# Attention in a two-block fp32 model: transposed weight groups in pairs and in two banks, at four places of a round in place of eight

## The reference

```
for i in range(S // BLOCK_Q):                       # S = 512, BLOCK_Q = 128: four query blocks
    z = einsum('bhqd,bhkd->bhqk', qb, kb) * SB_SCALE  # keys 0 .. (i+1)*128
    log_1m_beta = where(mask, -softplus(z), 0.0)
    suffix = cumsum(log_1m_beta, reverse) - log_1m_beta
    w = where(mask, exp(log_sigmoid(z) + suffix), 0.0)
    outs.append(einsum('bhqk,bhkd->bhqd', w, vb))
p_a = (attn * silu(z_a)) @ w_branch_a
```

## Time and profile before

| what | value |
|---|---|
| median of 3 runs | 1523.73 us (1523.71 to 1523.83) |
| the profiled execution, its own time | 1523.92 us |
| its span, first to last instruction | 1522.2 us |
| TensorE matmul busy | 1507.5 us, 99% of the span |
| VectorE, ScalarE busy | 1014.8 us (67%), 713.3 us (47%) |
| attention rounds | from about 977.8 to 1215.3 us of the span |
| length of one looped round | 29.78 us (first score matmul of a round at 1036.51, of the next at 1066.29) |

### The profile page before, as it was taken

The page is one execution under the profiler, slowest core; times in us unless marked ns, Lnnn a source line. Parts: engine busy times, 40 slices in busy tenths (PEclk is TensorE's granted clock), DMA queues, the critical chain, the costliest instruction groups (busy, mean ns, idle before and its releaser), DMA issues.

```text
span 1522.2 us, 22929 instructions
## 1 busy us (share of the span) xinstructions
PE 1507.5 (99%) x8868; PEld 1334.1 (88%) x8868; DVE 1014.8 (67%) x1206; ACT 713.3 (47%) x1045; POOL 54.3 (4%) x101
## 2 busy tenths in 40 slices
PE   8999999999999999999999999999999999999998
PEld 7899998889888889899999888788888888888887
DVE  5888884327856848888886675688888775323243
ACT  6545443226566327544443324566766633312234
POOL 1000000002100002000000001000000000000001
PEclk9999999999999999999999999999999999999999
DMA  6233324322332231333325762232322222332321
GB/s 197 84 112 107 97 73 139 105 88 84 85 95 75 83 111 56 111 98 98 104 89 221 232 208 57 56 84 55 83 66 72 81 85 84 112 110 84 109 83 56
DMA packets 134909, 153.23 MB, mean 101 GB/s; under 512 B 3600, under 2 KB 123532, under 8 KB 134844
## 3 DMA queue, kind: packets, MB, share of 16 engines
q1 hardware_dynamic: 131584, 137.38, 28.8%
q0 software_dynamic: 3024, 14.88, 2.9%
q10 hardware_dynamic: 236, 0.06, 0.0%
HBM read 150.08 MB, written 2.23 MB: 100 GB/s over the span
## 4 chain that ended last, share of the span: by engine, by line
PE 96%; DVE 2%; ACT 1%; issue 0%; DMA 0%; DVEq 0%; ACTq 0%
PE ps L2305 21%; PE ps L2307 21%; PE ps L2306 21%; PE ps L2504 16%; PE ps L2509 8%; PE ps L2668 1%; PE ps L2769 1%; PE ps L2779 1%; PE ps L2753 1%; PE ps L2752 1%; PE ps L2778 1%; PE ps L2386 0%; PE ps L2735 0%; PE ps L2446 0%; DVE wl L1415 0%
## 5 line engine op out<-in xcount | busy, mean ns | idle before, releaser
L2305 PE MATMUL ps<-ah,wh 128*128 128x512 f32 (+1 forms) x1344 | 512.7, 381 | 3.1 <-DVE al L1469 1.2
L2307 PE MATMUL ps<-ah,wl 128*128 128x512 f32 (+1 forms) x1344 | 503.7, 375 | 0.0
L2306 PE MATMUL ps<-al,wh 128*128 128x512 f32 (+1 forms) x1344 | 503.1, 374 | 0.0
L2305 PEld LDWEIGHTS ps<-ah,wh 128*128 128x128 f32 x1344 | 253.4, 189 | 49.5 <-issue 2.3
L2307 PEld LDWEIGHTS ps<-ah,wl 128*128 128x128 f32 x1344 | 252.9, 188 | 46.0
L2306 PEld LDWEIGHTS ps<-al,wh 128*128 128x128 f32 x1344 | 253.4, 189 | 41.5
L1415 DVE TENSOR_TENSOR wl<-raw,wh 128x2048 fp32r<-128x2048 f32 x52 | 119.1, 2291 | 164.7 <-ACT wh L788 164.5
L788 ACT ACTIVATE wh<-raw 128x2048 fp32r<-128x2048 f32 x53 | 101.3, 1912 | 197.0 <-PE ps L2307 193.3
L2504 PE MATMUL ps<-ah,wh 128*128 128x256 f32 x576 | 141.3, 283 | 0.0
L2504 PE MATMUL ps<-al,wh 128*128 128x256 f32 x576 | 141.3, 283 | 0.0
L2504 PEld LDWEIGHTS ps<-al,wh 128*128 128x128 f32 x576 | 110.6, 192 | 0.1
(11 more groups left out here) (395 smaller groups left out, 2383.5 us busy)
## 6 DMA issues: line engine op xcount, KB each, us to landing
raw<-in_w_ffn_in SPq DMA_DIRECT2D x74, 512.0 KB, 3.5
raw<-in_w_ffn_out SPq DMA_DIRECT2D x22, 1024.0 KB, 5.0
raw<-in_w_in SPq DMA_DIRECT2D x36, 512.0 KB, 5.1
raw<-in_w_in SPq DMA_DIRECT2D x14, 1024.0 KB, 5.6
ada_raw<-in_w_ada POOLq DMA_DIRECT2D x8, 1536.0 KB, 7.1
raw<-in_w_mix_in SPq DMA_DIRECT2D x10, 1024.0 KB, 5.3
raw<-in_w_ffn_in SPq DMA_DIRECT2D x7, 1024.0 KB, 5.2
raw<-in_w_mix_out SPq DMA_DIRECT2D x4, 1024.0 KB, 4.9
```

The costliest lines, as they stand in the source:

```text
L2305: nc.tensor.matmul(bank, w[0], m[0], start=start, stop=False, skip_group_check=shared)
L2306: nc.tensor.matmul(bank, w[0], m[1], start=False, stop=False, skip_group_check=shared)
L2307: return nc.tensor.matmul(bank, w[1], m[0], start=False, stop=stop, skip_group_check=shared)
```

## The change

The transposed groups are done in pairs side by side. The two groups of a pair go to different banks, so neither waits for the other's reader: T(0,i) to banks 7, 6, 7, 6 (7 is the value bank of PV) and T(1,i) to banks 6, 4, 4, 6 (4 is a score bank). They stand at places 4, 7, 10 and 13 of a round, where before they stood at 4, 5, 7, 8, 10, 12, 13 and 15. On ScalarE and VectorE the copies stand in pairs too, ahead of `sz` and `zs` at place 7; at place 4 VectorE now does Q(0,3) first. The waits of the bank's readers are moved to fit: T(0,0) waits for the sum that reads bank 7, T(0,1) for V's last reader, T(1,1) for the sigmoids that read bank 4, and Q(0,0) for the last low part of the round before.

```diff
-ATT_PE = {0: [("Q", 0, 0), ("Q", 0, 1), ("PV", 1), ("V",)], 1: [("Q", 0, 2)], 2: [("Q", 0, 3)], 4: [("T", 0, 0), ("Q", 1, 0)],
-          5: [("T", 0, 1)], 7: [("Q", 1, 1), ("T", 0, 2), ("Q", 1, 2)], 8: [("T", 0, 3)], 9: [("Q", 1, 3)],
-          10: [("PV", 0), ("T", 1, 0)], 12: [("T", 1, 1)], 13: [("T", 1, 2)], 15: [("T", 1, 3)]}
+ATT_PE = {0: [("Q", 0, 0), ("Q", 0, 1), ("PV", 1), ("V",)], 1: [("Q", 0, 2)], 2: [("Q", 0, 3)], 4: [("T", 0, 0), ("T", 0, 1), ("Q", 1, 0)],
+          7: [("Q", 1, 1), ("T", 0, 2), ("T", 0, 3), ("Q", 1, 2)], 9: [("Q", 1, 3)],
+          10: [("PV", 0), ("T", 1, 0), ("T", 1, 1)], 13: [("T", 1, 2), ("T", 1, 3)]}
...
-           4: [("T", 0, 0), ("hi", 0, 1), ("Q", 1, 0)], 5: [("T", 0, 1)], 7: [("T", 0, 2), ("sz",), ("Q", 1, 1)],
-           8: [("T", 0, 3), ("Q", 1, 2)], 9: [("Q", 1, 3), ("k own",), ("hi", 1, 0)], 10: [("T", 1, 0), ("hi", 1, 1)],
-           12: [("T", 1, 1), ("q own",), ("sum", 0)], 13: [("T", 1, 2), ("k other",)], 15: [("T", 1, 3)]}
+           4: [("T", 0, 0), ("T", 0, 1), ("hi", 0, 1), ("Q", 1, 0)], 7: [("T", 0, 2), ("T", 0, 3), ("sz",), ("Q", 1, 1)],
+           8: [("Q", 1, 2)], 9: [("Q", 1, 3), ("k own",), ("hi", 1, 0)], 10: [("T", 1, 0), ("T", 1, 1), ("hi", 1, 1)],
+           12: [("q own",), ("sum", 0)], 13: [("T", 1, 2), ("T", 1, 3), ("k other",)]}
...
-           4: [("T", 0, 0), ("Q", 0, 3)], 5: [("T", 0, 1), ("lo", 0, 1), ("Q", 1, 0)], 7: [("T", 0, 2), ("zs",), ("Q", 1, 1)],
-           8: [("T", 0, 3), ("Q", 1, 2)], 9: [("Q", 1, 3), ("gal",)], 10: [("T", 1, 0), ("lo", 1, 0)],
-           12: [("T", 1, 1), ("k low",), ("sum", 0)], 13: [("T", 1, 2), ("q low",)], 15: [("T", 1, 3), ("lo", 1, 1)]}
+           4: [("Q", 0, 3), ("T", 0, 0), ("T", 0, 1)], 5: [("lo", 0, 1), ("Q", 1, 0)], 7: [("T", 0, 2), ("T", 0, 3), ("zs",), ("Q", 1, 1)],
+           8: [("Q", 1, 2)], 9: [("Q", 1, 3), ("gal",)], 10: [("T", 1, 0), ("T", 1, 1), ("lo", 1, 0)],
+           12: [("k low",), ("sum", 0)], 13: [("T", 1, 2), ("T", 1, 3), ("q low",)], 15: [("lo", 1, 1)]}
+T_BANK = 7, 6, 7, 6, 6, 4, 4, 6
...
                     if idx == 0:
                         pe.wait_ge(qe_done, r * 3 + 3)
                         pe.wait_ge(ke_done, r + 1)
+                        pe.wait_ge(tlo_done, r * 8)
...
                     if idx == 0:
+                        pe.wait_ge(pv_sum, r * 2)
+                    elif idx == 1:
                         pe.wait_ge(vlo_done, r + 1)
+                    elif idx == 5:
+                        pe.wait_ge(sig_done, r * 8 + 7)
                     else:
-                        pe.wait_ge(tlo_done, r * 8 + idx)
+                        pe.wait_ge(tlo_done, r * 8 + {2: 1, 3: 2, 4: 4, 6: 6, 7: 5}[idx])
                     for b in range(i + 1):
-                        last = nc.tensor.transpose(ps[:, 6, b * P:(b + 1) * P], wt_of(i)[:, b * P:(b + 1) * P], ident[:])
+                        last = nc.tensor.transpose(ps[:, T_BANK[idx], b * P:(b + 1) * P], wt_of(i)[:, b * P:(b + 1) * P], ident[:])
```

More of the change, by code:

```diff
@@ L1222, in att_step @@
                     nc.scalar.activation(wTh[:, 0:i + 1, i * P:(i + 1) * P],
-                                         ps[:, 6, 0:(i + 1) * P].rearrange("p (b t) -> p b t", t=P), ACT.Copy).then_inc(thi_done, 1)
+                                         ps[:, T_BANK[idx], 0:(i + 1) * P].rearrange("p (b t) -> p b t", t=P), ACT.Copy).then_inc(thi_done, 1)
                 elif kind == "gah":
@@ L2097, in att_step @@
                     place = (slice(None), slice(0, i + 1), slice(i * P, (i + 1) * P))
-                    nc.vector.tensor_tensor(wTl[place], ps[:, 6, 0:(i + 1) * P].rearrange("p (b t) -> p b t", t=P),
+                    nc.vector.tensor_tensor(wTl[place], ps[:, T_BANK[idx], 0:(i + 1) * P].rearrange("p (b t) -> p b t", t=P),
                                             wTh[place].bitcast(fp32), ALU.subtract).then_inc(tlo_done, 1)
```

## The result

The changed kernel takes 1527.13 us, median of 13 runs (1527.00 to 1527.38), against 1523.73 us before (13 runs, 1523.61 to 1523.92): a ratio of 1.0022, 95% interval 1.0014 to 1.0031. It is 3.4 us slower; 4.5 us were forecast.

The account below looks back on a forecast made before the run. TensorE, busy 1507.5 of 1522.2 us, was taken to bound the kernel. Stalls of 3.9 us (looped) and 1.1 us (written-out rounds) less 0.5 us for `uS` gave +4.5 us: median 1528.2 us, range 1525.3 to 1530.5 us.

Parts of the forecast that it names:

- The stall at place 8 in the looped rounds: TensorE waits for `zs`, delayed by T(0,3)'s copies: 0.71 us, net 0.65 a round, 3.9 us over six rounds.
- a chain of links: Behind T(0,3)'s start at place 7: high part at +0.63, low part at +1.26, `zs` at +1.86 us.
- The stall in the two written-out rounds: Place 8 of the rounds outside the loop: loss 0.53 us each, 0 before, 1.1 us together.
- a release of 0.05 us: Delay from the end of `zs` to TensorE's weight load in written-out rounds, taken from `uS`; the loop shows 0.23 us.
- these 0.3 us: T(0,3) in the last round lost 0.3 us before, no releaser named; it may vanish under the stall or not.
- The wait for `uS`: Behind the last round, TensorE's 0.49 us stall goes because T(1,3) at place 13 frees ScalarE earlier.
- The pairing: On TensorE, the same 20 transposes a round at 0.11 us each: no gain and no loss.
- a place has a fixed price: Rival: each switch of place costs 0.09 us, so four fewer save 2.9 us, giving 1525.3 us; chance 0.05.
- The Trainium skill's 81 ns: TensorE's transposes could reach 81 ns in longer runs, giving back 4.6 us (1523.6 us); the trace showed 110 ns.
- Waits on another bank than before cost nothing where they are long met: TensorE's moved bank waits cost nothing; the round's head, behind `q low`, has 1.3 us to spare.
- `zs` being hidden: Rival: nothing is lost at place 8, the bank 3 wait stays hidden, 1522.9 us; chance 0.10.
- the second wait at the head of a round: Rival: the head waits for `q low` if place 13's chain is 1.3 us longer; 1532.2 us; chance 0.06.

Follow-up runs that it names:

- Experiment 1: The changed kernel with `sz` and `zs` ahead of T(0,2) and T(0,3) at place 7 on ScalarE and VectorE; 1521.44 us.
- experiment 3: The kernel before the change with `sz` and `zs` ahead of T(0,2) at place 7, nothing else; 1523.07 us.
- experiment 4: The kernel before the change with only T(0,2) and T(0,3) paired at place 7, ahead of `sz` and `zs`, T(0,2) in bank 7; 1528.61 us.
- experiment 6: The changed kernel with `sz` and `zs` moved further back, behind Q(1,1)'s work at place 7; 1535.63 us.
- experiment 9: Experiment 1's kernel with T(1,3) back at place 15 on all three engines, still in bank 6; 1525.35 us.
- experiment 11: Experiment 10's kernel with Q(0,0) waiting for T(1,2)'s low part, bank 4's last reader, not T(1,3)'s; 1523.78 us.
- experiment 12: Experiment 9's kernel with Q(0,0) waiting for T(1,2)'s low part, bank 4's last reader, not T(1,3)'s; 1522.80 us.
- Experiment 8: Experiment 1's kernel with scores Q(0,3) directly behind Q(0,2) at place 1 on TensorE; 1521.62 us.
- experiment 7: Experiment 1's kernel with two long-met waits on TensorE at each of places 5, 8, 12 and 15; 1521.43 us.
- experiment 10: The kernel before the change with the changed kernel's banks and waits, every group at its old place; 1526.18 us.
- experiment 5: The changed kernel with TensorE, at the head of a slot, waiting for its low weights before the gate instead of after; 1526.47 us.

## Why the prediction was right, and where its sizes were off

The direction, the place and the mechanism were right, and the time lay in the range. That it lay 1.1 us under the forecast has two causes, the pairing and a wait that was already there in the last round; a slightly longer stall worked against them. Experiment 1 is the change without its stall, so it parts the terms:

- **The stall at place 8 in the looped rounds.** Forecast 0.71 us, less the 0.06 that was lost before, 0.65 net, from a chain of links out of the earlier trace rows. The links measured 0.63, 1.27 and 1.88 us where 0.63, 1.26 and 1.86 were forecast, and the stall is 0.72 us to the second weight matmul and 0.76 over the whole round (30.30 against 29.55 in experiment 1). Before, 0.07 us were lost (experiment 3). So 0.69 net, 4.1 us in six rounds where 3.9 were forecast. The table's 2.12 - (0.94 + 0.53) = 0.65 us is less, because it has a part of the pairing's gain in it. Experiments 4 (this pair alone) and 6 (make it longer) bear it out.
- **The stall in the two written-out rounds.** Forecast 0.53 us each with "it was 0 before", 1.06 in all, with a release of 0.05 us. The release measured 0.07 and 0.06. In round 0 the stall is 0.56 us (29.36 against 28.80 us for the round in experiment 1). In the last round it is 0.59 (extra of places 7 and 8: 1.96 against 1.37), but there 0.26 us had been lost before: "0 before" was read from the earlier trace rows, which is round 0, while in the last round TensorE waited for `zs` ahead of T(0,3) (experiment 3). The prediction saw these 0.3 us and left their cause open. Sum 0.9 us.
- **The wait for `uS`.** Forecast -0.49 us, and it is gone. After, there is no wait for it, and the places around it have no extra; experiments 4, 9, 11 and 12, with T(1,3) at place 15, all have it, and 1, with T(1,3) at place 13, has not.
- **The pairing, mis-sized.** Forecast 0: "no gain and no loss". Experiment 1's looped round is 0.21 us shorter than that of the kernel before; less the 0.07 us for `zs`, the pairing gives 0.14 us a looped round, 0.10 in round 0 and some 0.2 in the last, 1.1 us in all. So the sum is 4.1 + 0.9 - 0.5 - 1.1 = 3.4 us, as measured. The step that was off is the reading of the earlier trace rows to the second weight matmul only. To there it holds after as well: three and four transposes cost 0.33 and 0.44 us apart and 0.77 together. But each group of transposes costs a few hundredths more before the next place begins (0.37 and 0.47 apart, 0.78 together), and fewer groups pay that less often. The rival "a place has a fixed price" was right in kind and some two and a half times too large, with a mean of 0.035 us a place for its 0.09; places 10 and 12 gave nothing, 13 and 15 gave 0.06. Experiment 8 shows that it isn't a price of places as such, experiment 7 that it isn't one of waits. What about the transposes makes it stays open.
- **The Trainium skill's 81 ns** for a 128-column matmul in a stream ("TensorE: Matmul & The Clock Gate", Back-to-back issue gap) is not reached in a run of seven either: 0.78 us there is 0.11 us each, so this trace disagrees.
- **The banks.** "Waits on another bank than before cost nothing where they are long met" is right, but the prediction checked the wait added to Q(0,0) only in its new surroundings, by way of `q low`, which stands behind T(1,3)'s low part there. It is long met there only because T(1,3) came up from place 15 to 13. Two parts of the change thus hang together: the banks with the old places cost 2.1 us (experiment 10), with the wait aimed at the right reader nothing (experiment 11).

The other rivals: `zs` being hidden is out by the trace, and the second wait at the head of a round did not come. After, the head's scores start without idle time. The forecast owes something to luck all the same: the gain that it left out and the wait of the last round fell within a range that was drawn for the release and the links.

## What to carry to other kernels

When a step is grouped with its neighbour, look at what its readers now stand in front of on the other engines: here a gate of 0.7 us was pushed back by a copy that nobody needed yet, and moving it to the front of both lists made the same grouping 2.4 us faster than the original in place of 3.4 us slower. The price of the stall could be read ahead from one round, link by link, start to start, to some hundredths of a us; the busy share showed nothing. A round that is written out by itself can have its waits in another order, and has to be read by itself. A wait for a shared buffer should name the last reader of that buffer and not the last item of the series, or its price depends on where that item stands.

## What the runs showed of the hardware

- The delay from the end of VectorE's instruction to the weight load that waited for it is not one number. It was 0.23 us in a loop with another wait behind it that asks for another register value (0.24 in experiment 6), 0.11 us with that wait put ahead, in the loop and in round 0 (experiment 5), and 0.06 to 0.07 us where the waits are on constants (`zs` in round 0 and the last round after) or, in the loop, where the wait behind asks for the same register value (experiment 10). Behind ScalarE's `uS` it was 0.05 us.
- Eight more waits a round on TensorE that are already met cost nothing measurable (experiment 7: 1521.43 against 1521.44 us), between blocks where TensorE always has work queued.
- Transposes of fp32 data cost 0.24 us for two, 0.37 for three, 0.47 for four and 0.78 for seven, beyond the weight matmuls around them; two groups of scores put together gained nothing (0.84 against 0.83 us).
